# The five RMS norms of a hybrid backbone: sums of squares in four column groups, root and reciprocal on 128x128, spread by products with a repeated column of the identity

## The reference, cut to what matters

```
def _rms_norm(x, g, eps=NORM_EPS):
    xf = x.astype(jnp.float32)
    y = xf * lax.rsqrt(jnp.mean(xf * xf, axis=-1, keepdims=True) + eps)
    return y.astype(x.dtype) * g
...
for l in range(DEPTH):
    h = _rms_norm(x, norm1_g[l]) * (1.0 + sc1) + sh1        # norm (l, 0); hc likewise
    ... projection, attention, RWKV-7 scan, output projection ...
    h = _rms_norm(x, norm2_g[l]) * (1.0 + sc2) + sh2        # norm (l, 1)
    x = x + gt2 * _channel_mixer(h, ...)                    # dense SwiGLU, then top-2-of-8 experts
return _rms_norm(x, final_g)                                # norm (2, 0)
```

## Time and profile before

| | us |
|---|---|
| median of 3 runs | 2581.51 (2579.84 to 2581.87) |
| the profiled execution | 2582.96 |
| its span | 2581.1 |
| PE busy | 2403.9 (93%) |
| DVE busy | 1623.0 (63%) |
| ACT busy | 1174.1 (45%) |

### The profile page before, as it was taken

How to read it: one execution, slowest core, us unless ns; L and a number is a source line. 1 busy time by engine, 2 the same in 40 slices (tenths; PEclk the granted TensorE clock), 3 DMA queues, 4 the chain that set the end, 5 groups by cost and what they waited for, 6 DMA issues and landing times.

```text
span 2581.1 us, 47722 instructions
## 1 busy us (share of the span) xinstructions
PE 2403.9 (93%) x19861; PEld 1849.5 (72%) x19861; DVE 1623.0 (63%) x1820; ACT 1174.1 (45%) x1243; POOL 171.2 (7%) x260
## 2 busy tenths in 40 slices
PE   5999889987999999899789959999999999999998
PEld 2446389943888785556689748888888888888886
DVE  3474556444333333484455349898989898989897
ACT  3341422212222222443222137676767676767675
POOL 0000054300000000000444000000000000000000
PEclk9999999998999999999899979999999999999999
DMA  7221700052333225221000439898989898989897
GB/s 274 66 82 66 261 4 4 20 196 82 98 98 98 82 80 210 66 84 57 2 4 20 181 131 374 318 374 316 365 319 367 317 371 312 363 327 373 310 372 268
DMA packets 233285, 497.58 MB, mean 193 GB/s; under 512 B 9398, under 2 KB 78284, under 8 KB 226092
## 3 DMA queue, kind: packets, MB, share of 16 engines
q1 hardware_dynamic: 230960, 481.10, 51.6%
q10 hardware_dynamic: 2172, 14.20, 1.5%
HBM read 488.98 MB, written 6.29 MB: 192 GB/s over the span
## 4 chain that ended last, share of the span: by engine, by line
PE 86%; DVE 5%; ACT 3%; issue 3%; POOL 2%; DMA 1%; ACTq 0%; DVEq 0%; POOLq 0%
PE ps L551 17%; PE ps L553 17%; PE ps L552 17%; PE ps L628 11%; PE ps L825 10%; PE ps L544 7%; PE ps L579 2%; POOL tail L2158 2%; ACT weight_parts L1485 2%; PE ps L853 2%; PE ps L602 1%; PE ps L1101 1%; PE ps L984 1%; DVE tail L1931 1%; DVE tail L1885 1%
## 5 line engine op out<-in xcount | busy, mean ns | idle before, releaser
L2066 DVE TENSOR_TENSOR weight_parts<-front,weight_parts 128x2048 fp32r<-128x2048 f32 x336 | 767.8, 2289 | 85.2 <-ACT weight_parts L1485 84.6
L1485 ACT ACTIVATE weight_parts<-front 128x2048 fp32r<-128x2048 f32 x336 | 642.2, 1918 | 245.1 <-PE ps L553 245.0
L551 PE MATMUL ps<-weight_parts,token_parts 128*128 128x512 f32 x1344 | 533.8, 397 | 16.2 <-DVE token_parts L2073 16.2
L552 PE MATMUL ps<-weight_parts,token_parts 128*128 128x512 f32 x1344 | 526.3, 392 | 0.0
L553 PE MATMUL ps<-weight_parts,token_parts 128*128 128x512 f32 x1344 | 526.1, 391 | 0.0
L551 PEld LDWEIGHTS ps<-weight_parts,token_parts 128*128 128x128 f32 x1344 | 253.6, 189 | 71.8 <-DVE token_parts L2073 18.1
L1182 ACT ACTIVATE tail<-ps 128x512 f32<-128x512 f32 (+2 forms) x219 | 124.2, 569 | 393.8 <-DVE tail L1849 170.6
L628 PE MATMUL ps<-front,tail 128*128 128x512 f32 (+3 forms) x704 | 286.1, 563 | 12.4 <-ACT front L1256 7.6
L553 PEld LDWEIGHTS ps<-weight_parts,token_parts 128*128 128x128 f32 x1344 | 254.0, 189 | 54.8
L552 PEld LDWEIGHTS ps<-weight_parts,token_parts 128*128 128x128 f32 x1344 | 254.3, 189 | 51.0
L825 PE MATMUL ps<-tail 64*64 64x64 f32 x7808 | 258.1, 220 | 32.2 <-POOL tail L2158 15.4
(11 more groups left out here) (222 smaller groups left out, 2309.1 us busy)
## 6 DMA issues: line engine op xcount, KB each, us to landing
front<-in_exp_w SPq DMA_DIRECT2D x342, 1024.0 KB, 5.7
tail<-in_ffn_w SPq DMA_DIRECT2D x30, 1024.0 KB, 5.0
tail<-in_ada_w SPq DMA_DIRECT2D x27, 1024.0 KB, 8.7
tail<-in_w_in SPq DMA_DIRECT2D x24, 1024.0 KB, 5.1
front<-in_ada_w SPq DMA_DIRECT2D x21, 1024.0 KB, 8.9
tail<-in_w_out SPq DMA_DIRECT2D x8, 1024.0 KB, 5.1
parked_x<-front ACTq DMA_DIRECT2D x2, 2048.0 KB, 8.9
front<-parked_x ACTq DMA_DIRECT2D x2, 2048.0 KB, 9.3
```

The lines of the kernel that those rows point to most:

```text
L551: mm(view, a_hi, b_hi, start=start, stop=False)
L552: mm(view, a_lo, b_hi, start=False, stop=False)
L1485: f_(whi[k % PARTS], at(A_RING2 + (k % RING2) * SLOT2, SLOT2), ACT.Copy).then_inc(cnt["act"].sem, 1)
L2066: ins = v.tensor_tensor(wlo[m % PARTS], at(A_RING2 + (m % RING2) * SLOT2, SLOT2), whi[m % PARTS], ALU.subtract)
```

## The change

The sum of squares for one piece becomes one product for each block of 128 tokens (four, or two for 256 tokens), with a stationary operand of ones cut to 128x32. Each block writes its own strip of 32 partitions of the bank, columns 0 to 127. So the sums of 512 tokens lie in 128x128 numbers (those of 256 tokens in 64x128), each repeated over 32 partitions. The root and the reciprocal work on that. Then PE spreads the reciprocals: for block t, the stationary operand is column 32t of the identity repeated 128 times, the moving operand the reciprocals, and the product has row 32t of them on all partitions. The spread result lies in a PSUM bank of its own, and DVE scales from there. DVE waits for its last scaling to end before it releases the bank. In norm (0,0) PE does ada tiles 4 and 5 before it waits for the reciprocals (`norm_inv`), and tiles 6 and 7 after the spread. In the other norms the wait and the spread stand right behind the sums, in (0,1) and (1,1) ahead of `ada_turn`, in (1,0) behind the last ada tile.

```diff
--- before.py
+++ after.py
@@ -179,6 +179,9 @@
         eng.wait_ge(self.full[b], n)
         return self.psum[b]
 
+    def release(self, eng, key):
+        eng.sem_inc(self.free[self.where[key][0]], 1)
+
     def done(self, ins, key):
         ins.then_inc(self.free[self.where[key][0]], 1)
 
@@ -358,6 +361,9 @@
         sqm = at(A_HTOK, 4, LAT)
         rsm = at(A_HTOK + 1024, 2, LAT)
 
+        def rnorm_of(tag):
+            return (sqf[:, 4] if tag in ((0, 0), (0, 1), (1, 0)) else rsm[:, 0])[:, 0:P]
+
 
         loads = []
 
@@ -594,12 +600,15 @@
 
             def norm(tag, n0, sqv, w):
 
+                n_t = w // P
                 bank = banks.take(pe, ("norm", tag))
                 for c in range(DC):
                     if tag in ((0, 1), (1, 1)) and c >= 4:
                         ada_tile(3 + 2 * tag[0], c)
                     pe.wait_ge(ev("norm_sq"), DC * norm_no[tag] + c + 1)
-                    ins = mm(bank[:, 0:w], ones, sqv[:, c % 4, 0:w], start=(c == 0), stop=(c == DC - 1))
+                    for t in range(n_t):
+                        ins = mm(bank[32 * t:32 * t + 32, 0:P], ones[:, 0:32], sqv[:, c % 4, t * P:(t + 1) * P],
+                                 start=(c == 0), stop=(c == DC - 1), skip_group_check=True)
                     if c < DC - 1:
                         ins.then_inc(ev("norm_used"), 1)
                     if tag == (0, 0) and c < 4:
@@ -608,7 +617,16 @@
                         ada_tile(4, c // 2)
                 banks.fill(ins, ("norm", tag))
                 if tag == (0, 0):
-                    for k in range(4, DC):
+                    for k in range(4, 6):
+                        ada_tile(0, k)
+                pe.wait_ge(ev("norm_inv"), norm_no[tag] + 1)
+                bank = banks.take(pe, ("spread", tag))
+                for t in range(n_t):
+                    ins = mm(bank[:, t * P:(t + 1) * P], ident[0:32 * n_t, 32 * t:32 * t + 1].broadcast_to([32 * n_t, P]),
+                             rnorm_of(tag)[0:32 * n_t, :], start=(t == 0), stop=True, skip_group_check=True)
+                banks.fill(ins, ("spread", tag))
+                if tag == (0, 0):
+                    for k in range(6, DC):
                         ada_tile(0, k)
                     ada_turn(0)
                 elif tag in ((0, 1), (1, 1)):
@@ -1239,7 +1257,8 @@
                     if tag == (0, 1) and c >= DC - 1 - PARTS and c < DC - 1:
                         ffn_high(c - (DC - 1 - PARTS))
                 bank = banks.see(act, ("norm", tag))
-                banks.done(f_(srtv[:, 0:w], bank[:, 0:w], ACT.Sqrt, bias=epsc[NORM_EPS], scale=1.0 / D),
+                r = slice(0, w // 4)
+                banks.done(f_(rnorm_of(tag)[r, :], bank[r, 0:P], ACT.Sqrt, bias=epsc[NORM_EPS][r, :], scale=1.0 / D),
                            ("norm", tag))
                 if tag in ((0, 0), (0, 1), (1, 1)):
                     ada_row({(0, 0): 0, (0, 1): 3, (1, 1): 5}[tag])
@@ -1598,23 +1617,28 @@
                     for t in range(PARTS):
                         ffn_low(t)
                 banks.released(dve, ("norm", tag))
-                chain(v.reciprocal(rstv[:, 0:w], srtv[:, 0:w]))
+                v.reciprocal(rnorm_of(tag)[0:w // 4, :], rnorm_of(tag)[0:w // 4, :]).then_inc(ev("norm_inv"), 1)
                 if tag in ((0, 0), (1, 1)):
                     modulation(5 * tag[0])
                 l, n = tag
+                inv = banks.see(dve, ("spread", tag))
                 for c in range(DC):
                     if l == 2:
                         ins = v.scalar_tensor_tensor(xT[:, c, c0:NTOK], xT[:, c, c0:NTOK], vcol("final_g", c),
-                                                     rstv[:, 0:w], ALU.mult, ALU.mult)
+                                                     inv[:, 0:w], ALU.mult, ALU.mult)
                         continue
                     for s in (streams(l) if n else [0, 1]):
                         r = slice(s * CTX, (s + 1) * CTX)
                         ro = slice(s * CTX - c0, (s + 1) * CTX - c0)
                         ins = v.scalar_tensor_tensor(hT[:, c, r], xT[:, c, r], gain[:, 2 * l + n, c, s:s + 1],
-                                                     rstv[:, ro], ALU.mult, ALU.mult)
+                                                     inv[:, ro], ALU.mult, ALU.mult)
                     ins.then_inc(ev("h_scaled"), 1)
                 if l == 2:
                     ins.then_inc(ev("out_scaled"), 1)
+                    dve.wait_ge(ev("out_scaled"), 1)
+                else:
+                    dve.wait_ge(ev("h_scaled"), DC * (norm_no[tag] + 1))
+                banks.release(dve, ("spread", tag))
 
             def project(l):
                 t0 = first(l)
```

## The result

The changed kernel takes 2548.75 us (median of 4 runs, 2546.59 to 2554.77) against 2581.69 for the kernel before on the same chip: a ratio of 0.9869, interval 0.9852 to 0.9885. That is 33 us, where 19.5 were forecast, and it lies outside the range of 2557 to 2570. The profiled execution took 2550.38, its span is 2548.6.

A forecast was written before the change was run, and what follows sets the result against it. PE holds 86% of the chain, so time is won in the norms, where it works needlessly or idles. Terms 4.0 + 7.2 + 1.5 + 3.4 + 1.6 + 2.2 - 0.2 - 0.3 = 19.4 us: 2563.6 profiled, median 2562, range 2557 to 2570.

The forecast's parts named there:

- at least 12: Time from first sum to first scaling, added over five norms, must fall this many us, or the forecast is wrong.
- the signs of being wrong: Four sums at 2 us or more; PE waiting for ada tiles; spread at 2 us; projection behind (1,0) at 9.6.
- the rivals: Half overlap 0.12; no overlap 0.04; port and clock unchanged 0.08; gain lost to a transfer 0.05; slower, strips serial 0.03.
- The extra bank shifts the turn of the banks only until the explicit banks of the rates: PSUM bank order: the spread's bank is asked for again two products later, when scaling is over; no cost given.
- (0,0): Norm (0,0): faster pairs 2.8 and last sums 2.6, less 1.4 for the spread: net gain 4.0 us, bounds 1.5 and 5.
- (1,0): Norm (1,0): sums and tiles gain 5.8, root and reciprocal less spread 1.4: together 7.2 us, bounds 4.5 and 7.5.
- The clock term, 1.5: Projection behind norm (1,0): shorter PE idle time brings back between nothing and 2.7 us; 1.5 taken.
- (0,1): Norm (0,1): scaling starts 3.4 us earlier; the 16 scalings, one operand now from PSUM, gain 1.6 if freed from contention.
- (1,1): Norm (1,1): sums gain 3.0, order behind them loses 0.6, scaling from PSUM 0.2: net 2.2 us, bounds 0.2 and 2.7.
- the small losses that I had counted 0.5: Norm (2,0) -0.2 us, and DVE's new wait before the release of the bank -0.3 in all.

The follow-up runs named there:

- fullsums: Changed kernel with sums of squares as before (128x512 or 128x256, no column groups) and four or two short roots: 2581.79 us, ratio 0.9985 to the kernel before.
- spread1: Changed kernel, but norm (1,0)'s spread takes bank 1 by name and the turn goes on as if none were taken: 2559.8 us, ratio 0.9893.
- longwait: Changed kernel with four more 128x128 reciprocals behind the first in norm (1,0), so PE waits longer there: 2558.87 us, ratio 0.9905 to the kernel before.

## Why the prediction was wrong

The direction and most mechanisms were right: strips at full overlap (0.22 a piece, I said 0.24), reciprocals of 0.95, a spread of 1.16 (1.07), root behind the table load in (2,0), DVE waiting for the turn in (1,1), no instruction of 900 ns. The sum over the five norms fell by 20.6 us, where the forecast wanted at least 12. Of the signs of being wrong one came in part: the spread took 2.08 us in (0,1). None of the rivals came.

- **The step that failed** is the last sentence of the norm-by-norm part: "The extra bank shifts the turn of the banks only until the explicit banks of the rates". I costed it at nothing, and looked only at whether the spread's own bank would be asked for too early. The sentence itself is true, but "only until" is where the time lies. What the shift does to the product that shared its bank with the ada tiles I did not ask. The bank alone is worth 6.7 us in the profile of the kernel before, 6.6 in that of the changed one, and 10.6 (7 to 14) by runs. With it, the forecast would have been a gain of about 26, a median of about 2555.5: still some 7 us above what was measured. The rest is in the terms below and in the clock.
- **(0,0)**, 4.0: mis-sized, 5.4 at an equal clock. The four pairs save 3.9 at full clock, not 2.8. I had taken half clock and waits as a reason to count less for each pair; the profile of the kernel before shows the contrary, as its four pairs, partly at half clock, took 9.8 us where those at full clock take 8.2, and the new ones 4.3. The last sums, the tiles and the spread behind them gave 1.5 for 1.2. Of the 6.8 in the first pair of profiles 1.4 are clock and start. The medians give 8.4 for this norm; the difference is within the spread of the runs.
- **(1,0)**, 7.2: 7.5 and 7.4 by the lead in the two profiles. The clock term, 1.5: 0.8 and 2.5.
- **(0,1)**, 3.4 + 1.6 = 5.0: 6.2 and 5.6 by the lead from 604 to 700. The spread was dearer (2.08), scaling gave 2.4 instead of 1.6, more than the 1.8 that I had as its most.
- **(1,1)**, 2.2: 2.8 at the first scaling. But 2.7 are lost right behind it, at the router, where the granted clock is 0.52 for 0.63 (below). The kernel with the old (1,0), which has the new (1,1), does not lose them, nor do the one with the other three norms as before and the one with the long sums (fullsums).
- **The attention of layer 1**, no term: 4.9 gained between 1229 and 1270, 3.1 by its end.

For the last two the windows show the clock, not the cause. First the attention in the kernel before, then in the changed one, over the same instructions:

```profile
1228.40:1264.90 36.50, 24.26 (x282) 19.56 (x281) 12.47 (x27) 11.19 (x25) 14.21 (x21) 0.72 0.00 1
```

```profile
1197.60:1229.20 31.60, 18.97 (x281) 15.91 (x281) 12.30 (x25) 10.77 (x25) 13.84 (x20) 0.89 0.01 2
```

and then the router in the changed kernel and in the one with the old (1,0):

```profile
1464.50:1481.10 16.60, 10.27 (x48) 10.21 (x48) 3.42 (x11) 6.97 (x13) 0.00 (x0) 0.52 0.71 252
```

```profile
1474.50:1488.00 13.50, 7.18 (x48) 7.12 (x48) 3.42 (x10) 6.97 (x13) 0.00 (x0) 0.63 0.64 218
```

In the attention that is about 20 us at half clock before and 7 after. The gain there goes with norm (1,0): 4.7 to 4.9 in seven profiles with its new form, 2.6 in two more (the other three norms as before; the tiles moved into the waits), and nothing in the four with the long sums there. It is not the banks, which the kernel with the old (1,0) has as the changed one. It is not how early the stretch begins either: with a lead of 23.7 and 21.8 two kernels gain (spread1, longwait), with 23.8 the one with the old (1,0) does not. The length of the wait was tried and is not it. How a norm 220 us earlier goes with the clock there was not found, and with one or two profiles of each kernel it may be chance in part. Nor was it found why the router's loss is missing where either (1,0) or (1,1) is as before or has its long sums; what is lost there lies in 32 records of 128x8 in the router, which take 6.83 us in the changed kernel and 3.74 in the one with the old (1,0).

The account of the profiled execution, from the first column of the table: (0,0) and its projection 8.5, the first attention 1.0, (0,1) and its mixer 4.8, (1,0) 7.5 and its projection 0.8, the stretch of the bank 8.2, the second attention 3.1, (1,1) 2.8, the router -2.7, behind it -1.4: 32.6, and the spans differ by 32.5. Against the 19.4 of the forecast 13.2 are over. The stretch of the bank is 8.2 of them (6.6 the bank), (0,0) 4.5 (1.4 of it a term too small, most of the rest clock), the attentions 4.1, (1,1) 0.6, the small losses that I had counted 0.5; router, end, (0,1) and (1,0) take 4.7 back. So the bank is the largest cause, and it is shown; clock that fell otherwise makes up most of the rest, in both directions, and its cause stays open.

## What to carry to other kernels

Where buffers are handed out in turn, one more request renames every buffer behind it. List what each product got before and after, and ask who releases it, up to the next place where names are fixed: here a wait of 3.4 us, and the half clock behind it, hung on a counter. Look most closely where a buffer leaves a set of reserved ones, as it is then the next to be handed out. When cutting products into column groups, count the change of tile shape against the neighbours too: sums and ada tiles of one width run on without the 0.17 us a change that a full-width sum between them costs (2.05 a pair, where sum and tile alone take 0.855 and 0.87). And do not read a gain of 2 to 3 us out of one profile: the same code differed by 1.6 to 2.8 us in (0,0) alone. Compare a stretch between profiles in which its granted clock is the same.

## What the runs showed of the hardware

Four strips of 32 columns with only 128 moving columns each still run fully at once: 27 ns a record (0.87 us for 32 records). A copy of 128x512 from PSUM takes 0.69. The same spread takes 1.16 us behind 0.6 us of idle time (granted clock 1.00), 2.08 behind 2.25 and 2.07 behind 4.57 (0.50 in both). And the granted clock falls at different places in executions of the same code. The changed kernel from 43 to 52, in the projection behind (0,0), had 1.00 in one profile and this in the other:

```profile
43.00:52.00 9.00, 9.00 (x18) 3.74 (x18) 4.69 (x13) 6.88 (x15) 0.00 (x0) 0.81 0.47 180
```
